# A decoder layer in float32 on one core: the embedding product kept in DRAM until the tail, its first four tiles made at the start, a reordered ring of weight slots, and mixed activations rounded into ring slots

## What is computed

```python
xn = rmsnorm(h, norm1_g)
c_val, c_gate, l_x, l_gate = split(xn @ w_in + b_in)          # 2048 -> 4 x 1024
c  = silu(layernorm(causal_conv31(c_val * sigmoid(c_gate))))
r  = rg_lru(causal_conv4(l_x)) * gelu(l_gate)
h  = h + concat(c, r) @ w_out                                   # 2048 x 2048
h  = h + hier_moe(rmsnorm(h))       # top 1 of 4 groups, top 2 of its 8 experts; 32 experts, 2048 x 512 x 3
gate = sigmoid(rmsnorm(h) @ w_pg + b_pg)                        # 2048 x 2048
h  = h + gate * (p @ w_ple)                                     # p: 264 x 256, w_ple: 256 x 2048
y  = rmsnorm(h, final_g)
```

## Time and profile before

| | us |
|---|---|
| three runs, median (lowest to highest) | 1497.18 (1496.87 to 1504.12) |
| profiled execution, its own time | 1504.26 |
| profiled execution, span of its instructions | 1502.6 |
| TensorE busy | 1388.1 (92% of the span) |
| VectorE busy | 609.2 (41%) |
| ScalarE busy | 227.6 (15%) |
| moved from DRAM, over the span | 479.43 MB, 321 GB/s |

### The profile page before, as it was taken

How to read it: one execution, slowest core, us unless ns; L and a number is a source line. 1 busy time by engine, 2 the same in 40 slices (tenths; PEclk the granted TensorE clock), 3 DMA queues, 4 the chain that set the end, 5 groups by cost and what they waited for, 6 DMA issues and landing times.

```text
span 1502.6 us, 19007 instructions
## 1 busy us (share of the span) xinstructions
PE 1388.1 (92%) x7574; PEld 802.1 (53%) x7574; DVE 609.2 (41%) x1030; ACT 227.6 (15%) x368; POOL 40.8 (3%) x56
## 2 busy tenths in 40 slices
PE   7999998899999999999999989998999999997996
PEld 6888887799853333333333333333333333333995
DVE  5689643544443223223222322322232223226764
ACT  2000155633200000000000000000000000004552
POOL 0000000000000000000000000000000000000000
PEclk9999999999999999999999999999999999998998
DMA  9553230254559999999999999999999999998431
GB/s 391 218 207 132 112 121 1 85 197 169 202 233 389 421 422 422 422 422 422 422 421 422 422 422 422 422 422 422 422 422 422 422 422 422 422 421 346 140 140 59
DMA packets 68186, 482.45 MB, mean 321 GB/s; under 512 B 8176, under 2 KB 8208, under 8 KB 10528
## 3 DMA queue, kind: packets, MB, share of 16 engines
q1 hardware_dynamic: 66816, 478.93, 77.8%
q0 software_dynamic: 320, 1.59, 0.3%
q10 hardware_dynamic: 1008, 1.34, 0.3%
HBM read 479.43 MB, written 3.49 MB: 321 GB/s over the span
## 4 chain that ended last, share of the span: by engine, by line
PE 53%; DMA 41%; DVE 2%; ACT 2%; issue 1%; SPq 1%; DVEq 0%; ACTq 0%
DMA ring<-in_w_up_dram 39%; PE ps L608 15%; PE ps L791 14%; PE ps L663 4%; PE ps L813 4%; PE ps L664 4%; PE ps L665 4%; PE ps L824 2%; DMA p_late<-in_p_dram 1%; DMA ring<-in_w_down_dram 1%; SPq L460 1%; PE ps L751 1%; DVE hT L1518 1%; PE ps L617 1%; PE ps L752 1%
## 5 line engine op out<-in xcount | busy, mean ns | idle before, releaser
L791 PE MATMUL ps<-ring,xwin 128*64 128x512 f32 x1984 | 452.6, 597 | 40.3 <-DMA ring<-in_w_up_dram 40.3
L1518 DVE TENSOR_TENSOR hT<-hT,ps 128x1056 f32<-128x1056 f32 x128 | 160.5, 1254 | 376.3 <-PE ps L824 375.3
L791 PEld LDWEIGHTS ps<-ring,xwin 128*64 128x64 f32 x1984 | 146.0, 136 | 300.3 <-issue 257.7
L813 PE MATMUL ps<-ring,hid 128*64 128x512 f32 x1024 | 232.1, 606 | 17.1 <-DVE hid L1498 16.6
L608 PE MATMUL ps<-xT,ring 128*128 128x264 f32 x1024 | 233.9, 391 | 3.4 <-DVE xT L1162 3.4
L608 PEld LDWEIGHTS ps<-xT,ring 128*128 128x128 f32 x1024 | 197.6, 193 | 38.4 <-issue 3.8
L813 PEld LDWEIGHTS ps<-ring,hid 128*64 128x64 f32 x1024 | 71.8, 139 | 153.6 <-issue 130.9
L824 PE MATMUL ps<-S,ysb 64*128 64x264 f32 x1024 | 148.3, 408 | 1.3 <-issue 0.8
L824 PEld LDWEIGHTS ps<-S,ysb 64*128 64x128 f32 x1024 | 88.4, 186 | 110.9 <-issue 102.3
L1066 ACT ACTIVATE sgl<-ps 64x512 f32<-64x512 f32 x32 | 18.9, 590 | 579.0 <-PE ps L791 579.0
L1162 DVE SCALAR_TENSOR_TENSOR mix<-U,vT,mix 128x256 f32<-128x256 f32 x240 | 95.3, 479 | 0.0
(11 more groups left out here) (265 smaller groups left out, 1013.7 us busy)
## 6 DMA issues: line engine op xcount, KB each, us to landing
ring<-in_w_gate_dram SPq DMA_DIRECT2D x128, 1024.0 KB, 23.4
ring<-in_w_up_dram SPq DMA_DIRECT2D x128, 1024.0 KB, 25.4
ring<-in_w_down_dram SPq DMA_DIRECT2D x128, 1024.0 KB, 24.3
ring<-in_w_in_dram SPq DMA_DIRECT2D x32, 1024.0 KB, 7.5
ring<-in_w_out_dram SPq DMA_DIRECT2D x16, 1024.0 KB, 4.9
ring<-in_w_pg_dram SPq DMA_DIRECT2D x16, 1024.0 KB, 5.1
hT<-in_x_dram SPq DMA_DIRECT2D x4, 528.0 KB, 5.2
out_y_dram<-hg SPq DMA_DIRECT2D x4, 528.0 KB, 2.9
```

The lines of the kernel that those rows point to most:

```text
L791: mm = pe.matmul(ps[part * WIN:(part + 1) * WIN, 0, :], window(k), weights(2 * j + part)[:, kk * F:(kk + 1) * F], start=(k == 0), stop=(k ...
L813: mm = pe.matmul(ps[half * WIN:(half + 1) * WIN, 2 + b, :], hid[:, t, :], weights(8 + t)[:, q * 512:(q + 1) * 512], start=(t == 0), stop=( ...
L1518: dve.tensor_tensor(group(hT, g), group(hT, g), ps[:, bank:bank + 4, 0:TOK].rearrange("p (h k) t -> p h k t", h=2), ALU.add)\
```

## The change

- **Head.** SP loads p and the first quarter of w_ple (512 columns) right behind x. TensorE makes four tiles of the embedding product behind the row sums, ScalarE copies them and stores them to a new DRAM tensor `ple_dram`. The rest of w_ple is loaded into slots 4 and 5 at once, so w_in has the eight slots of IN_SLOT.
- **Mix.** ScalarE makes the squares one tile earlier (24 to 27). It rounds the weights of two tiles at tiles 28 and 29 and of the third behind all columns; the columns are rounded inside the step of tile 30, ahead of tile 31's Gelu. `x_hi` lies in slots 6 and 7, its last column in `I`. VectorE's order is changed to match.
- **Middle.** The twelve tiles of the embedding product go to three buffers (`ple_stage`), from which SP stores them to `ple_dram`. `hp_lo` lies where `pleT` was. SP loads expert 0's chunks in one go: eight as before, two when the output product is done, and behind the twelve stores the last two, when the embedding product is done; expert 1 follows as slots come free.
- **Tail.** The late loads, products and copies go. SP reads the whole product back into `pleT` behind the fourth tile of w_pg; VectorE waits for that ahead of the first multiplication.

```diff
-EXP_SLOT = [8, 0, 9, 1, 10, 2, 11, 3, 4, 5, 6, 7]
-REST_SLOT = 6
+EXP_SLOT = [8, 0, 9, 1, 10, 2, 11, 3, 6, 7, 4, 5]
+IN_SLOT = [8, 9, 0, 1, 10, 11, 2, 3]
+MIX_SLOT = 6
 PLE_SLOT = 4
 MIX_ORDER = list(range(TC, KD - 1)) + list(range(TC)) + [KD - 1]
 
...
-TAIL_LO = [8, 9, 10, 11, 4, 6]
-TAIL_HI = [0, 1, 2, 3, 5, 7]
+TAIL_LO = [8, 9, 10, 11, 6, 4]
+TAIL_HI = [0, 1, 2, 3, 7, 5]
...
-PLE_LATE = KD - PLE_FRONT
+PLE_HEAD = KD - PLE_FRONT
+PLE_STAGE = 3
...
-    x_hi = place("x_hi", [P, KD, TOK], F32R, r_xt)
+    x_hi = place("x_hi", [P, KD - 1, TOK], F32R, r_ring + MIX_SLOT * 8192)
+    x_hi_last = place("x_hi_last", [P, TOK], F32R, r_x + 20864)
+    hp_lo = place("hp_lo", [P, 2, KD, P], F32R, r_xt)
     pleT = place("pleT", [P, KD, TOK], F32, r_xt)
...
-    hp_lo = place("hp_lo", [P, 2, KD, P], F32R, r_ring + REST_SLOT * 8192)
     hp_few = place("hp_few", [P, 4, P], F32, r_x + 16384)
     rs = place("rs", [P, NSLOT], F32, r_x + 18432)
+    ple_head = place("ple_head", [P, PLE_HEAD, TOK], F32, r_x)
+    ple_stage = place("ple_stage", [P, PLE_STAGE, TOK], F32, r_x + 20544)
...
+    p_head = place("p_head", [P, 2, TOK], F32, r_free + 3168)
...
+    ple_dram = nc.dram_tensor("embedding_rows", (KD, P, TOK), F32, kind="Internal").ap()
...
-    def freed(n):
-
-        return n + 1 if n < CT_OUT else n + 1 - KD
...
+    def mix_hi(k):
+        return x_hi[:, k, :] if k < KD - 1 else x_hi_last[:, :]
...
     def slot(n):
-        return n % NS
+        return IN_SLOT[n % len(IN_SLOT)]
...
     def expert_count(j):
 
-        return 16 + slot_count(max(n for n in range(CH_IN) if slot(n) == EXP_SLOT[j]))
+        return 16 + (slot_count(CH_IN - 1) if EXP_SLOT[j] in IN_SLOT else 0)
+
+    def all_spilled(i):
+        return 16 * len(range(i, PLE_FRONT, PLE_STAGE))
...
         def load(n):
-            if n >= NS:
-                sp.wait_ge(*used(n - NS))
+            if n >= len(IN_SLOT):
+                sp.wait_ge(*used(n - len(IN_SLOT)))
             sp.dma_start(ring[:, slot(n), :], a["w_in"][n]).then_inc(slot_loaded[slot(n)], 16)
...
         for q in range(XQ):
             sp.dma_start(hT[:, 4 * q:4 * q + 4, :], a["x"][:, 4 * q:4 * q + 4, :]).then_inc(x_loaded[q], 16)
             if q == 1:
                 sp.dma_start(vT[:, :], a["vecs"][:, :]).then_inc(vec_loaded, 16)
+        sp.dma_start(p_head[:, :, :], a["p"][:, :, :]).then_inc(head_loaded, 16)
+        for k in range(CH_PLE):
+            sp.dma_start(ring[:, PLE_SLOT + k, 0:PLE_HEAD * P], a["w_ple"][k, :, 0:PLE_HEAD * P]).then_inc(head_loaded, 16)
         for m in range(4):
             load(m)
...
+        for k in range(CH_PLE):
+            sp.dma_start(ring[:, PLE_SLOT + k, PLE_HEAD * P:], a["w_ple"][k, :, PLE_HEAD * P:]).then_inc(ple_loaded, 16)
         for n in range(8, CH_IN):
             load(n)
...
         for t in range(KD):
             if t < PG_SLOTS:
-                sp.wait_ge(*used(CH_IN - NS + t))
+                sp.wait_ge(*used(max(n for n in range(CH_IN) if slot(n) == lo_slot(t))))
             else:
                 sp.wait_ge(acc_full, CT_OUT + t - PG_SLOTS + 1)
-            if t == 2 * PG_SLOTS:
-                for k in range(CH_PLE):
-                    sp.dma_start(ring[:, PLE_SLOT + k, :],
-                                 a["w_ple"][k]).then_inc(ple_loaded, 16)
             load_tile(t)
...
         for j in range(10):
             s = EXP_SLOT[j]
-            if s in (PLE_SLOT, PLE_SLOT + 1):
-                sp.wait_ge(acc_full, CT_PG)
-            else:
-                sp.wait_ge(acc_full, CT_PLE - PG_SLOTS + s % PG_SLOTS + 1)
+            sp.wait_ge(acc_full, CT_PLE - PG_SLOTS + s % PG_SLOTS + 1 if j < 8 else CT_PLE)
             load_chunk(0, j)
-        for j in range(8):
-            sp.wait_ge(*used_expert(0, j))
-            load_chunk(1, j)
-        sp.wait_ge(slots_full, 8)
+        for m in range(PLE_FRONT):
+            sp.wait_ge(ple_taken, m + 1)
+            sp.dma_start(ple_dram[PLE_HEAD + m], ple_stage[:, m % PLE_STAGE, :]).then_inc(ple_out[m % PLE_STAGE], 16)
+        sp.wait_ge(acc_full, CT_PG)
         for j in (10, 11):
             load_chunk(0, j)
-        for j in range(8, CH_EXP):
+        for j in range(CH_EXP):
             sp.wait_ge(*used_expert(0, j))
             load_chunk(1, j)
...
@@ -498,6 +507,11 @@
             else:
                 sp.wait_ge(acc_full, CT_PG + m - TAIL_SLOTS + 1)
             load_tile(KD + m)
+            if m == 3:
+                sp.wait_ge(head_out, 16)
+                for i in range(PLE_STAGE):
+                    sp.wait_ge(ple_out[i], all_spilled(i))
+                sp.dma_start(pleT[:, :, :], ple_dram.rearrange("m p t -> p m t")).then_inc(ple_back, 16)
...
@@ -588,8 +602,10 @@
 
             if CT_OUT <= n - 3 < CT_PLE:
                 pe.wait_ge(h1_ready, n - 3 - CT_OUT + 1)
+            elif n - 3 >= CT_PLE:
+                pe.wait_ge(ple_taken, n - 3 - CT_PLE + 1)
...
                     ch = chunk0 + k
-                    w = ring[:, PLE_SLOT + k, (n - CT_PLE) * P:(n - CT_PLE + 1) * P]
+                    m = PLE_HEAD + n - CT_PLE
...
             mm = pe.matmul(ps[:, 0, 0:TOK], ones[:, :], xT[:, k, :], start=(k == 0), stop=(k == KD - 1))
         mm.then_inc(row_full, 1)
 
+        pe.wait_ge(head_loaded, 16 * (CH_PLE + 1))
+        for m in range(PLE_HEAD):
+            for k in range(CH_PLE):
+                mm = pe.matmul(ps[:, 4 + m, 0:TOK], ring[:, PLE_SLOT + k, m * P:(m + 1) * P], p_head[:, k, :],
...
 
             if j == 0:
...
@@ -660,9 +685,9 @@
                 if t % KD == 0:
                     pe.wait_ge(ready, i + 1)
                 w_hi, w_lo = ring_r[:, hi_slot(t), k, :], ring_r[:, lo_slot(t), k, :]
-                pe.matmul(out, w_hi, hi[:, k, :], start=(i == 0), stop=False)
+                pe.matmul(out, w_hi, hi(k), start=(i == 0), stop=False)
                 pe.matmul(out, w_hi, rest[:, k, :], start=False, stop=False)
...
                 pe.wait_ge(h1_ready, m - 2)
             else:
...
@@ -761,7 +786,7 @@
 
         def spread_scale():
 
-            pe.wait_ge(acc_free, freed(CT_PG - 1))
+            pe.wait_ge(ple_taken, PLE_FRONT)
             pe.wait_ge(rstd_split, 1)
             for half in range(2):
                 cols = slice(half * TOK, (half + 1) * TOK)
@@ -883,23 +908,15 @@
         for g in range(4):
...
-        for i in range(PLE_LATE):
-            for k in range(CH_PLE):
-                mm = pe.matmul(ps[:, 4 + i, 0:TOK], w_late[:, k, i * P:(i + 1) * P], p_late[:, k, :],
-                               start=(k == 0), stop=(k == CH_PLE - 1))
-            mm.then_inc(late_full, 1)
 
         for m in range(KD):
             if m == 0:
                 pe.wait_ge(main["added"], 4 * E + 1)
             if m >= 3:
                 pe.wait_ge(scaled_out, m - 2)
-            split_product(KD + m, CT_PG + m, SC_ORDER, z_hi, z_lo, z_lo_ready)
...
                 for i in range(4):
                     mm = pe.matmul(ps[:, 5, 0:TOK], ones[:, :], acc4[:, i, :], start=(i == 0), stop=(i == 3))
                 mm.then_inc(row_full, 1)
@@ -928,6 +945,12 @@
             act.activation(xT[:, 4 * q:4 * q + 4, :], hT[:, 4 * q:4 * q + 4, :], ACT.Square).then_inc(x_squared, 1)
         act.wait_ge(ms_ready, 1)
         act.activation(rb[:, :], rb[:, :], ACT.Sqrt).then_inc(root_ready, 1)
+
+        for m in range(PLE_HEAD):
+            act.wait_ge(head_full, m + 1)
+            act.activation(ple_head[:, m, :], ps[:, 4 + m, 0:TOK], ACT.Copy).then_inc(head_taken, 1)
+        act.wait_ge(head_taken, PLE_HEAD)
+        act.dma_start(ple_dram[0:PLE_HEAD].rearrange("m p t -> p m t"), ple_head[:, :, :]).then_inc(head_out, 16)
...
+
+        def round_mix(j):
+            act.activation(mix_hi(j), mix[:, j, :], ACT.Copy).then_inc(mix_hi_ready, 1)
...
-            if 25 <= n < 29:
-                p = n - 25
+            if 24 <= n < 28:
+                p = n - 24
                 for j in range(2 * p, 2 * p + 2):
                     act.wait_ge(centred, j + 1)
                     if p:
                         act.wait_ge(sq_used, p)
                     act.activation(sq[:, j % 2, :], mix[:, j, :], ACT.Square).then_inc(sq_ready, 1)
-            if n == 30:
+            if n in (28, 29):
+                round_weights(n - 28)
+            if n == 29:
                 act.wait_ge(var_ready, 1)
                 act.activation(I[:, 1, :], I[:, 0, :], ACT.Sqrt).then_inc(sd_ready, 1)
-            if 28 <= n < 31:
-                round_weights(n - 28)
-
-        def silu(j):
-            act.wait_ge(scaled, j + 1)
-            act.activation(mix[:, j, :], mix[:, j, :], ACT.Silu, scale=vT[:, V_LNG + j:V_LNG + j + 1],
-                           bias=vT[:, V_LNB + j:V_LNB + j + 1]).then_inc(mixc_ready, 1)
-
-        for j in MIX_ORDER:
-            if j < TC:
-                if j == 0:
-                    silu(0)
-                if j + 1 < TC:
-                    silu(j + 1)
-                act.wait_ge(mixc_ready, j + 1)
```

(53 more changed lines are left out.)

34 lines of the change are left out of this document (21 added, 13 removed).

## The result

The changed kernel takes 1490.01 us (median of 6 runs, 1489.10 to 1490.66). The kernel before, timed beside it, takes 1503.78 us in the median of all its 6 runs: the three shown ahead of the prediction (1496.87, 1504.12, 1497.18) and three more (1503.80, 1504.19, 1503.76). The ratio on record is 0.9925, 95% interval 0.991 to 0.994, which is 9 to 13.5 us of 1503.78: faster and clear of noise, though by less than one per cent. The two medians differ by 13.8 us, more than the interval holds, because the six runs of the kernel before lie in two groups, two near 1497 and four near 1504. I had predicted 1482.3 us, from a gain of 14.9 us. In the profiled executions the gain is 1504.26 - 1490.41 = 13.85 us; for one like the profiled one I had put 1489.4 us.

The account below looks back on a forecast made before the run. Weight transfers were taken to bound the experts, TensorE and its waits the rest. 2.1 + 9.5 − 0.4 + 3.7 = 14.9 us gain gave 1489.4 from the profiled 1504.26, 1482.3 us from the median 1497.18; range 1476 to 1491.

Parts of the forecast that it names:

- The step that failed: Whole kernel: profiled execution stands 7.1 us above the runs' median 1497.18, so 1489.4 for one like it becomes 1482.3 us.
- Head: At the start: added embedding matmuls fill TensorE's pause, leaving none for the clock to fall in; gain 2.1 us.
- Mix: Up to the last mixed column: earlier squares and rounding remove TensorE's stall and shorten ScalarE's chain; gain 9.5 us.
- Middle: Embedding product to experts: stores put the gather 1.5 us later, two chunks load earlier; net 0.4 us lost.
- The 1.1 us that I had credited to the two early chunks: Middle: the gain from loading expert 0's chunks 10 and 11 earlier, without the gather's 1.5 us delay.
- the 1.7 us of a lone load: Middle: estimated part, ahead of the data, of the 2.4 us beyond the data in a lone load's 4.9 us.
- Tail: Behind the experts: without late products the first gate tile starts after the last scatter's addition; gain 3.7 us.
- (1): Expert transfers: the full ring pays, two chunks shift the stream by all of 5.0 us; 1478.4 us, chance 0.10.
- (2): Mix: ScalarE is the bound, seven table switches add 9.0 us, the mix gains only 0.5; 1491.3 us, chance 0.12.
- (3): Middle: stores serialise the embedding product, net loss 3l − 8.2 us for landing l; 1503.4 us at 9.9, chance 0.05.
- the 9.9 us that I had named: Middle: upper bound for a store's landing, from the RG-LRU tail's 44 KB store; 1.9 us was taken instead.
- the 4 us that I had given as a sign of being wrong: Middle: embedding product stores landing later than 4 us would show the forecast wrong.

Follow-up runs that it names:

- no_head: The changed kernel without its 16 matmul passes of the embedding product at the start; 1489.13 us.
- before_fill_half: The kernel before with 14 and 16 filler passes in two TensorE pauses, behind the row sums and ahead of the third variance pair; 1499.46 us.
- woven: The changed kernel with the first two output tiles interleaved, so other columns run ahead of the first tile's last column; 1487.59 us.
- before_no_late: The kernel before with the late embedding product's loads, wait, eight products and copies left out; 1500.48 us.
- before_again: The kernel before, unedited, run once more for a second profile; 1501.91 us, its profiled execution 1501.10 us.

## Why the prediction was right and wrong

**The step that failed** is the last one: "it stands 7.1 us above the median of the runs, 1497.18, from which I get 1482.3 us". I took the gain from an execution at 1504 and subtracted it from one at 1497. A part of the gain exists only in the former. The clock was down there from 18.0 to 24.9 us and from 243.3 to 250.1, behind the two pauses that the change removes. By the passes run at the lower level that is 2.75 us at the head (29.42 less 26.54 less 0.13) and 2.5 in the mix (tile 29 in 8.73 us instead of 7.28, the variance pair in 2.13 instead of 1.1): 5.2 of my 14.9. no_head shows that an execution without the fall loses nothing at the head. Without these 5.2 us the profiles leave 8.6 of the 13.85. Against the runs at 1497 the change brings 7 us, against those at 1504 some 14. The 70 runs of the kernel before have their median at 1501.8 us (20 below 1500, 25 from 1500.7 to 1502.7, 25 above 1503), the 12 of the changed kernel at 1490.6: 11.3 us. The runs of the kernel before under 1499 us have a mean granted clock of 0.986 to 0.990, those above 1503 one of 0.980 to 0.984, where it is listed. That a run near 1497 has neither of the two falls is argued from these clocks and from before_fill_half; none of them was profiled. I had the spread of the three runs in front of me, and explained the clock's fall as something that a pause brings about each time.

**The terms**, measured from first profile to first profile. *Head*, 2.1: it measured 2.88, all but 0.13 of it clock. I had taken 50.30 us for the end of four tiles, but that row ends with the question, at 50 us, and holds 126 of their 128 passes; the fourth tile's evacuation starts at 50.78 us, and the same sum would have given some 0.45 us more. That the passes fill the pause was right, and so was the cover of ScalarE's copies and the store. *Mix*, 9.5: at the last column it measured 9.3, tile 31 at 261.68 where I said "near 262", the column at 270.35 where I said 270.5. But at the end of the output product only 7.97 of it were left. What I missed is what is late next: TensorE had reached the last column 2.03 us early, and the clock fell in that wait; the passes that follow ran at the lower level until 273.7 us. woven, which takes the wait away, gets 3.76 us back. *Middle*, -0.4: -0.23 up to expert 0, and 0.06 up to the last chunk; that the sum is near is luck. The gather started 23.77 us behind the token squares instead of 22.23, 1.5 us later as I had put it, but the kernel before then had its clock down from 414.0 to 417.4 us, and the changed kernel's first profile has no such fall; in its second, which has one, the way from the token squares to expert 0 is 35.46 us instead of 34.03. The 1.1 us that I had credited to the two early chunks did not come. The stores were near what I priced: with one buffer the wait is 1.83 us where I took 1.9 for a landing, with three the median from issue to landing is 2.7; the 1.7 us of a lone load in that sum no run shows. *Tail*, 3.7: 3.83, and before_no_late shows 3.64 for the same edit alone. The read back landed 21.5 us after its issue, not 5.1, behind four chunks in the same queue; it was issued at 1352.03 us and first wanted at 1390.63, so nobody waited.

**The rivals.** (1) The full ring does not pay: with the two chunks held back the experts take the same 895.1 us. The idle stretch ahead of expert 0's down product is there as predicted, with a transfer share of 0.52 and 0.26. (2) ScalarE is not slowed by its tables: each of the loads takes 1.28 us, the instruction behind it starts 0.01 to 0.02 us later and the one ahead of it ends 0.02 us earlier, as in the rows of the mix above (259.26, 267.19). The Trainium skill (ScalarE: Activation LUTs, What ACT_TABLE_LOAD costs) adds a drain of 1.38 us to each; no row here shows it, so the measurement stands. (3) The stores don't serialise the product with three buffers; with one they do, by 16.8 us. A wait near the 9.9 us that I had named is seen only for the first store, behind four chunk loads: 8.0 us with one buffer. That is over the 4 us that I had given as a sign of being wrong, but my sum had this store wait for those loads.

**What stays open.** Why one and the same pause is followed by a fall in one execution, by a shorter one in another and by none in a third is not settled. The first tile starts at times that differ by 1.3 us among the four in the table, although the row sums ahead of it all start at 5.79 to 5.85 us: they take 10.02, 8.74, 9.85 and 9.04 us, as TensorE's passes become faster at different times (6 passes from 8 to 10 us in the first profile, 9 in the second). No run here separates that from other causes. A stall of 4.09 us at the variance without a fall was not seen in any of the profiles.

## What to carry to other kernels

A profile is one execution: a gain that hangs on TensorE's clock behind a pause is worth only the share of executions in which the clock falls there, so take the base and the gain from the same execution, and look at the spread of the runs before subtracting. A term that comes out right in one pair of profiles can still hide two errors, or a fall that only one of the two has. When a wait is removed, work out which engine arrives early at the next one; here a new pause of 2.03 us and the fall behind it ate 1.3 of the 9.3 us that the reordering had brought, and weaving the next tile into it gave 3.76 us. Count passes in the trace, not products in the code, before filling a pause.

## What the runs showed that I had not expected

- The same pause of 3.44 us at the start was followed by a clock of 0.72 on the mean of 16 to 28 us, by 0.86, and by 1.00, in three profiled executions (before, before_again, no_head); a fourth (before_no_late, the kernel before up to its tail) had it down from 18.0 to 24.8 us, like the first.
- Filling two pauses kept the clock up there, and in the profiled execution it fell at two later ones instead (before_fill_half, 0.70 from 270 to 280 us and 0.52 from 410 to 420).
- Filler of ones times ones ahead of the first gate tile, 4.21 us for 18 passes of 128 columns, ran at the lower level to its end; the clock was up 1.4 us later.
- A store of 135 KB is waited for 1.83 us when the queue is otherwise empty, and the first one, behind four chunks of 1 MB, is waited for 8.01 us.
